# Computing the values of two dilated attention groups with the tokens stationary, in place of transposing them

## The reference, cut to what matters

```python
proj = h @ w_in                                   # h: 512 x 1024
qa, ka, va, za, qr, kr, vr, zr, ga, gr = jnp.split(proj, SPLIT_POINTS, axis=-1)
att_shape = (B, S, N_ATT_GROUPS, ATT_HEADS_PER_GROUP, ATT_HEAD_DIM)   # 3 groups, 4 heads, 128
...
for g, (window, dil) in enumerate(ATT_PATTERNS):  # (128,1), (512,4), (2048,16)
    o, lse = dilated_window_attention(qa[:, :, g], ka[:, :, g], va[:, :, g], window, dil)
```

## Time and profile before

| | before |
|---|---|
| median of 3 runs | 2590.46 us (2588.53 to 2593.51) |
| the profiled execution: time | 2593.51 us |
| the profiled execution: span, first to last instruction | 2591.7 us |
| granted TensorE clock, mean | 0.994 |
| busy: TensorE matmuls | 2564.2 us (99%), 13376 instructions |
| busy: weight loads | 2170.9 us (84%), 13376 instructions |
| busy: VectorE, ScalarE, GpSimd | 1157.5, 1045.2, 1135.2 us (45%, 40%, 44%) |

### The profile page before, as it was taken

One profiled execution on the slowest core, in us unless ns is written; L12 is line 12 of the kernel. 1 busy time (PEld: TensorE's weight loads), 2 busy tenths in 40 slices (PEclk: granted clock), 3 DMA queues, 4 the chain that ended last, 5 costly groups with the idle time before them and its releaser, 6 DMA issues.

```text
span 2591.7 us, 33239 instructions
## 1 busy us (share of the span) xinstructions
PE 2564.2 (99%) x13376; PEld 2170.9 (84%) x13376; DVE 1157.5 (45%) x2373; ACT 1045.2 (40%) x2006; POOL 1135.2 (44%) x663
## 2 busy tenths in 40 slices
PE   8999999999999999999999999999999999999998
PEld 8888877778888888889888888888898888888887
DVE  6572466556432694101333354542142345544313
ACT  3462376763234433223443333333243333333322
POOL 3354344444445455445344444444444444444342
PEclk9999999999999999999999999999999999999999
DMA  5133210105533354223222222222222222222222
GB/s 189 66 102 105 72 33 25 34 25 195 195 106 138 109 192 167 96 95 105 78 82 82 82 80 83 86 86 98 98 99 88 83 84 79 88 82 83 96 94 87
DMA packets 71769, 250.47 MB, mean 97 GB/s; under 512 B 7872, under 2 KB 12736, under 8 KB 71232
## 3 DMA queue, kind: packets, MB, share of 16 engines
q1 hardware_dynamic: 71616, 248.35, 28.4%
HBM read 246.22 MB, written 2.10 MB: 96 GB/s over the span
## 4 chain that ended last, share of the span: by engine, by line
PE 93%; DVE 4%; ACT 2%; DMA 0%; issue 0%; POOL 0%; DVEq 0%; SPq 0%
PE bank L1714 91%; PE bank L1724 3%; DVE XC L2241 1%; DVE rk_lo L2233 0%; DVE Ylo L2233 0%; DVE sq L2233 0%; ACT TR L1939 0%; ACT w_hi L1939 0%; DVE nt L2233 0%; DMA w_raw<-in_wa 0%; DVE Hlo L2233 0%; DVE nB L2233 0%; ACT Hhi L1939 0%; DMA XR<-in_x 0%; DVE blkk L2237 0%
## 5 line engine op out<-in xcount | busy, mean ns | idle before, releaser
L2769 POOL TENSOR_TENSOR w_lo<-w_raw,w_hi 128x1024 fp32r<-128x1024 f32 (+1 forms) x398 | 949.6, 2390 | 1137.7 <-ACT w_hi L1939 1137.3
L1714 PE MATMUL bank<-Hhi,w_hi 128*128 128x512 f32 (+1 forms) x2144 | 844.0, 394 | 1.4 <-DVE XC L2241 1.3
L1714 PE MATMUL bank<-Hlo,w_hi 128*128 128x512 f32 (+1 forms) x2144 | 825.0, 385 | 2.2 <-DVE Hlo L2233 0.8
L1714 PE MATMUL bank<-Hhi,w_lo 128*128 128x512 f32 (+1 forms) x2144 | 824.2, 384 | 0.0
L1939 ACT ACTIVATE w_hi<-w_raw 128x1024 fp32r<-128x1024 f32 (+1 forms) x398 | 408.0, 1029 | 163.1 <-DMA w_raw<-in_wa 118.1
L1714 PEld LDWEIGHTS bank<-Hhi,w_lo 128*128 128x128 f32 x2144 | 404.5, 189 | 81.3
L1714 PEld LDWEIGHTS bank<-Hhi,w_hi 128*128 128x128 f32 x2144 | 405.1, 189 | 79.8 <-issue 5.3
L1714 PEld LDWEIGHTS bank<-Hlo,w_hi 128*128 128x128 f32 x2144 | 405.5, 189 | 72.3 <-DVE Hlo L2233 3.0
L1714 PE MATMUL bank<-w_hi,Hhi 128*128 128x256 f32 (+2 forms) x384 | 117.6, 306 | 0.0
L1714 PE MATMUL bank<-w_hi,Hlo 128*128 128x256 f32 (+2 forms) x384 | 116.0, 302 | 0.0
L1714 PE MATMUL bank<-w_lo,Hhi 128*128 128x256 f32 (+2 forms) x384 | 115.9, 302 | 0.0
(11 more groups left out here) (355 smaller groups left out, 4264.6 us busy)
## 6 DMA issues: line engine op xcount, KB each, us to landing
w_raw<-in_wb SPq DMA_DIRECT2D x211, 512.0 KB, 3.4
w_raw<-in_wa SPq DMA_DIRECT2D x174, 512.0 KB, 3.4
wm<-in_w_ada SPq DMA_DIRECT2D x48, 512.0 KB, 4.4
wa_raw<-in_wb SPq DMA_DIRECT2D x5, 512.0 KB, 6.0
XR<-in_x SPq DMA_DIRECT2D x4, 512.0 KB, 6.5
w1k<-in_w1k SPq DMA_DIRECT2D x1, 2048.0 KB, 12.8
w1v<-in_w1v SPq DMA_DIRECT2D x1, 2048.0 KB, 17.7
XR<-in_x SPq DMA_DIRECT2D x1, 2048.0 KB, 8.3
```

What stands on the lines that cost most here:

```text
L1714: return self.e.matmul(o, lhs, rhs, start=start, stop=stop)
L2769: self.e.tensor_tensor(x.lo[:, k:k + n, :], x.raw[:, k:k + n, :], f(x.hi[:, k:k + n, :]), ALU.subtract).then_inc(*w_rest(s, k))
```

## The change

The values of groups 1 and 2 of a head are computed together by `product_t`, with 128 tokens of `H` stationary and the 256 weights of both groups moving. The stationary tokens are taken at a step of four, `x[:, r:512:4]`, which is a step of 16 bytes, so that the result of place r has the tokens r, r+4, ... on its partitions. The existing `in_rows` (`rows_split`) rounds it with ScalarE and subtracts with VectorE, straight from the bank to `vB12`. Group 0 keeps its product, copy and transposes. In the weights' layout the two tiles of one k now lie side by side. The values of the two groups have one signal, `("v12", L, hh, 3)`, where they had two.

```diff
-        def dilated_values(self, L, hh, H, free):
-            for g in (1, 2):
-                self.run(self.product(H, ("bv", L, hh, g), self.turned_to(L, hh, g, free)))
...
                 i2 = hh % 2
-                v_free = self.v_free[i2]
+                v12 = [vB12[i2][:, :, x, :, :].rearrange("p g t n -> p t g n") for x in range(2)]
+                dilated = self.product_t(H, ("v12", L, hh), 256, PAIRS,
+                                         self.in_rows(("v12", L, hh), *(lambda t, v=v: v[:, t, :, :] for v in v12), self.v_free[i2]),
+                                         lambda x, r: x[:, r:512:4])
                 if hh:
-                    self.dilated_values(L, hh, H, v_free)
+                    self.run(dilated)
                 for g in range(3 if hh else 0):
                     self.run(self.product(H, ("bk", L, hh, g), self.to_k(L, hh, g)))
                 for g in range(0 if hh else 1, 3):
                     self.run(self.product(H, ("bq", L, hh, g), self.to_q(L, hh, g)))
                 if hh == 0:
-                    self.dilated_values(L, hh, H, v_free)
-                self.run(self.product(H, ("bv", L, hh, 0), self.turned_to(L, hh, 0, v_free)))
+                    self.run(dilated)
+                self.run(self.product(H, ("bv", L, hh), self.turned_to(L, hh, self.v_free[i2])))
...
         def att_times_dilated(self, L, hh, x, k, ob, bank_free):
-            self.wait_ge(act_att.by("t", L, hh, x), dve_att.by("t", L, hh, x), dve_att.by("vt", L, hh, 1), dve_att.by("vt", L, hh, 2), bank_free)
+            self.wait_ge(act_att.by("t", L, hh, x), dve_att.by("t", L, hh, x), dve_att.by("v12", L, hh, 3), bank_free)
...
-        def v_copy(self, L, hh, g, i, o, points):
+        def v_copy(self, L, hh, i, o, points):
             self.wait_ge(*points)
-            if g == 0:
-                self.put(vfB[i][:, :], o).then_inc(*act_att("v", L, hh, g))
-            else:
-                self.put(vfB[i][:, :].rearrange("p (r t) -> p r t", r=4), o.rearrange("p (t r) -> p r t", r=4)).then_inc(
-                    *act_att("v", L, hh, g))
+            self.put(vfB[i][:, :], o).then_inc(*act_att("v", L, hh))
...
             kq, v = [x[h::4] for x in (ka, qa)], va[h::4]
-            v = [v[1:3]]
+            v = [v[1:3].transpose(1, 0, 2, 3)]
```

More of the change, by code:

```diff
@@ L1126, in in_rows, with turned_to @@
             return evac
-        def turned_to(self, L, hh, g, *points):
+        def turned_to(self, L, hh, *points):
             def evac(o, done, c):
@@ L1131, in evac @@
                 self.n_vf += 1
-                self.v_copy(L, hh, g, i, o, [done, self.vf_free[i]])
+                self.v_copy(L, hh, i, o, [done, self.vf_free[i]])
                 def turn():
@@ L1136, in turn @@
                     b = self.tb_.take()
-                    self.v_turn(L, hh, g, i, b, self.freed[b], points)
-                    self.vf_free[i] = att_turned.by("v", L, hh, g)
-                    self.freed[b] = [dve_att.by("vt", L, hh, g)]
+                    self.v_turn(L, hh, i, b, self.freed[b], points)
+                    self.vf_free[i] = att_turned.by("v", L, hh)
+                    self.freed[b] = [dve_att.by("v0", L, hh)]
                     yield 0
                 self.turns.append(self.later(turn()))
-                return [act_att.by("v", L, hh, g)]
+                return [act_att.by("v", L, hh)]
             return evac
-        def dilated_values(self, L, hh, H, free):
-            for g in (1, 2):
-                self.run(self.product(H, ("bv", L, hh, g), self.turned_to(L, hh, g, free)))
         def silu(self, key, dst, *points):
@@ L1630, in stat_parts @@
         return st, st[:, 96:104], st[:, 104:112], st[:, 112:120]
-    def value_rows(hh, g):
-        if g == 0:
-            return vB[hh % 2][0][:, :, :], vB[hh % 2][1][:, :, :]
-        return vB12[hh % 2][:, g - 1, 0, :, :], vB12[hh % 2][:, g - 1, 1, :, :]
     def dilated_sums(b, r):
@@ L1848, in cmp_times, with v_turn @@
             self.mm(o, vc[rows, gp, :], ct_lo[v % 2][rows, :], False, True).then_inc(*valued.named(*names))
-        def v_turn(self, L, hh, g, i, b, bank_free, points):
-            self.wait_ge(act_att.by("v", L, hh, g), bank_free)
+        def v_turn(self, L, hh, i, b, bank_free, points):
+            self.wait_ge(act_att.by("v", L, hh), bank_free)
             for s in range(TT):
                 ins = self.transpose(banks[b][:, 128 * s:128 * s + 128], vfB[i][:, 128 * s:128 * s + 128])
-            ins.then_inc(*att_turned("v", L, hh, g))
+            ins.then_inc(*att_turned("v", L, hh))
         def att_qk(self, L, hh, n, b, first, final, bank_free):
@@ L1892, in att_times_near @@
             i2, c = hh % 2, 0
-            self.wait_ge(act_att.by("t", L, hh, x), dve_att.by("vt", L, hh, 0), bank_free, dve_att.by("t", L, hh, x))
+            self.wait_ge(act_att.by("t", L, hh, x), dve_att.by("v0", L, hh), bank_free, dve_att.by("t", L, hh, x))
             for g, s, have in PACKS[x]:
@@ L2154, in rows_split, with v_turn @@
             self.put(hi, banks[b][:, :].rearrange("p (t g n) -> p t g n", t=2, g=2)).then_inc(*act_att(*key, t))
-        def v_copy(self, L, hh, g, i, o, points):
+        def v_copy(self, L, hh, i, o, points):
             self.wait_ge(*points)
-            if g == 0:
-                self.put(vfB[i][:, :], o).then_inc(*act_att("v", L, hh, g))
-            else:
-                self.put(vfB[i][:, :].rearrange("p (r t) -> p r t", r=4), o.rearrange("p (t r) -> p r t", r=4)).then_inc(
-                    *act_att("v", L, hh, g))
-        def v_turn(self, L, hh, g, i, b, bank_free, points):
-            self.wait_ge(att_turned.by("v", L, hh, g), *points)
-            self.put(value_rows(hh, g)[0], banks[b][:, :].rearrange("p (s n) -> p s n", s=TT)).then_inc(*act_att("vt", L, hh, g))
+            self.put(vfB[i][:, :], o).then_inc(*act_att("v", L, hh))
+        def v_turn(self, L, hh, i, b, bank_free, points):
+            self.wait_ge(att_turned.by("v", L, hh), *points)
+            self.put(vB[hh % 2][0][:, :, :], banks[b][:, :].rearrange("p (s n) -> p s n", s=TT)).then_inc(*act_att("v0", L, hh))
         def silu2(self, key, dst, o, points):
@@ L2611, in rows_split, with v_turn @@
             self.tt(lo, banks[b][:, :].rearrange("p (t g n) -> p t g n", t=2, g=2), f(hi), ALU.subtract).then_inc(*dve_att(*key, t))
[L2613 to L2616, removed]
+        def v_turn(self, L, hh, i, b, bank_free, points):
+            hi, lo = vB[hh % 2]
+            self.wait_ge(act_att.by("v0", L, hh))
+            self.tt(lo[:, :, :], banks[b][:, :].rearrange("p (s n) -> p s n", s=TT), f(hi[:, :, :]), ALU.subtract).then_inc(*dve_att("v0", L, hh))
         def silu2(self, key, dst, o, points):
```

## The result

The changed kernel takes 2674.43 us (median of 4 runs, 2674.21 to 2677.66) where the kernel before takes 2591.93 (4 runs, 2588.53 to 2593.51). The ratio is 1.0323, with a 95% interval of 1.0305 to 1.0341: slower by 82.5 us. The forecast was 2587, the range ended at 2642. Rival A's upper price, 2664, comes nearest.

A forecast was written before the change was run, and what follows sets the result against it. TensorE, busy for 99% of the span, was taken as the bound. Removed transposes, -7.2 us, and more but shorter matmuls, +3.8, gave -3.4 us: from the median of 2590.46 to 2587, range 2583 to 2642.

The forecast's parts named there:

- Rival A: Dilated values' `product_t`: the load at 16 bytes becomes TensorE's bound, +37 us (2627) or +74 (2664); 34 in 100.
- I take the contiguous price: New product's weight loads at a 16-byte step: as fast as contiguous ones, 0.113 us, hidden behind 256 columns at 0.120.
- The 0.78 ns an element: VectorE's reads of `Ek` at 32 bytes: at most this, against 0.88 ns a column that a load needs.
- The rows of `tmpB`: Reads and writes at 16 bytes by other engines: slower by 1.52 on VectorE, 1.95 for ScalarE's writes.
- the 0.007 us of margin: New product on TensorE: a load slot of 0.113 us hidden behind a matmul of 256 columns, 0.120 us.
- a rule that spoke against the change: Trainium skill on SBUF's 16-byte lines: readers need at least two hits a line; a 16-byte step gives one.
- -7.2 for the turns: Groups 1 and 2, 8 heads: 16 transposes of values (`v_turn`) removed from TensorE at 0.447 us each.
- +3.8 for the halved matmuls: Per head, 96 matmuls of 256 columns at 0.120 us replace 48 of 512 at 0.2264 or 0.2313.
- Nothing for ScalarE, VectorE, the slabs and banks 6 and 7: Work beside TensorE counted 0: ScalarE mostly idle, slabs keep their pace, the new banks have 5.4 us of air.
- Rival C: New product: fewer transpose pieces only open gaps for waits on banks 6 and 7; 2590 to 2594 us; 4 in 100.
- Rival B: First retention head of each layer: TensorE's waits for a late low part go, -4.9 us, 2585.6; 19 in 100.
- What would show it: Changed profile: `vfB` transposes 96 to 32, 256 more `w_hi,Hhi` matmuls, starts 0.120 us apart; 0.17 to 0.22 if loads are slower.

The follow-up runs named there:

- step1: The changed kernel with 128 neighbouring tokens stationary (a step of 4 bytes) instead of every fourth, for timing alone: 2588.2 us, ratio 0.9992.

## Why the prediction was wrong

- **The step that failed** is "I take the contiguous price" for the load whose columns lie 16 bytes apart. The slot is 0.2333 us, 2.07 times the 0.113 of the earlier trace rows. Every nanosecond above 0.120 was to cost 0.77 us, and that price was right: 113.3 ns x 0.768 = 87.0 us. No other term of the sum was wrong by more than the measurement can tell.
- **Why that price was taken.** It came from another engine, and from a row that was misread. The 0.78 ns an element of the earlier trace rows takes the whole duration of a short operation, 0.17 us, from the distance between two long ones, 0.26. The records overlap (they last 0.33), so a distance holds less of the fixed part than a duration does. By durations throughout, `Ek` took (334 - 170) / 116 = 1.41 ns an element, and contiguous operands of the same kind of operation (261 - 178) / 168 = 0.49: 124 elements at 32 bytes lasted longer than 192 in a row. The pattern differs in more than its step (four runs of 31), so how much of this is the step's isn't shown. But the row was no evidence that a wide step is free, and it stood alone on that side. The rows of `tmpB` were set aside because a load doesn't write, but nothing showed that the writing was what cost there. Measured on TensorE itself, the load needs 1.82 ns a line and the moving side 0.87. VectorE's groups in the kernel before, the reads of `Ek` and two contiguous operations (count, busy us, mean ns):

```profile
L2237 DVE TENSOR_SCALAR blkk<-Ek,par 128x124 f32<-128x124 f32 x16 | 4.2, 334 | 0.0
L2238 DVE TENSOR_SCALAR gate<-gate 128x192 f32<-128x192 f32 x1 | 0.3, 261 | 0.3 <-ACT gate L1939 0.3
L2237 DVE TENSOR_SCALAR gh<-par 128x24 f32<-128x24 f32 x1 | 0.2, 178 | 1.9 <-DMA par<-in_par 1.9
```

- **How the chances were dealt.** The prediction had the place (the 0.007 us of margin), the asymmetry (a faster load gains nothing, a slower one costs 0.77 us per ns) and a rule that spoke against the change. With a gain of 3.4 us on one side and 37 to 74 on the other, the unknown was the whole forecast, and 34 in 100 for it was too little. The range then left out A's upper price, the one nearest the truth.
- **Rival A** had the mechanism: the load as the bound of `product_t`, in the 96 matmuls of each head. Its upper factor, 1.95, from ScalarE's writes to `tmpB`, gave a slot of 0.220 and 2664 us; measured were 0.233 and 2674. The factor is that of another engine's writes, and no run ties it to the load's 2.07, so that it came so near is luck as far as is known.
- **-7.2 for the turns and +3.8 for the halved matmuls** hold together: step1 has both and no slow load, and took 2588.2 against 2590.62, -2.4 us with an interval from -4.4 to 0, where -3.4 was forecast. They were not measured apart.
- **Nothing for ScalarE, VectorE, the slabs and banks 6 and 7**: right. The even distances of the changed kernel and of step1 show no idle time at the new product. Rival C falls.
- **Rival B** falls too. The wait of the earlier trace rows is still there, in the changed kernel's timeline as the line below (0.58 us), and costs 0.72 to 0.75 us a layer over the even distance in this kernel and in step1.

```profile
1567.36 0.48 PE L1707 MATMUL bank<-tB,vB_hi 128*128 128x256 f32 x2 [0.58 <-DVE tB L2222]
```

- **What would show it**: the distance was named as the deciding sign, 0.120 or 0.17 to 0.22. It was 0.233, at a clock of 1.00. The counts came as said; in the changed kernel's groups (busy us, mean ns) the matmuls `w_hi,Hhi` of 256 columns are 544, 256 more, and the pieces of `vfB` 32 in place of the 96 of the earlier trace rows:

```profile
L1707 PE MATMUL bank<-w_hi,Hhi 128*128 128x256 f32 x544 | 184.5, 339 | 0.0
L1717 PEld LDWEIGHTS bank<-ident,vfB 128*128 128x128 f32 x32 | 4.0, 139 | 1.0
```

## What to carry to other kernels

A stationary operand with a step of 16 bytes takes twice the time to load; behind a matmul of 512 columns that is free, behind one of 256 it doubles the distance: before a transpose is traded for a strided load, ask how many columns follow each load, and put it clear of another task's short matmuls. An operation that the profile doesn't show should be priced by a row of the same engine and the same port. If no such row exists and the margin is small, the forecast is that unknown, and a row from another engine shouldn't decide it. Any row used as a price should be set against its contiguous twin, durations with durations and distances with distances.

## What the runs showed of the hardware

- Time of a weight load of 128 columns by the step of its operand, as the distance of starts behind 256 columns: 4 and 8 bytes 0.120 (set by the columns; the load alone is 0.113), 12 bytes 0.177, 16 bytes 0.233, 32 bytes 0.242. From 12 bytes up that is 1.82 to 1.89 ns for each 16-byte line.
- The moving operand at 16 bytes: 0.87 ns a column against 0.42.
- Behind a short matmul of 128 columns, a matmul of 512 takes 0.29 to 0.30 us to the next start with a contiguous load, and 0.40 with one at 16 bytes.
- The rule of the Trainium skill ("Advanced Engine Details and Errata", section "SBUF Cachelines") shows in both of TensorE's operands, where the size differs. VectorE's read at 32 bytes lasted longer than a contiguous one as well (1.41 ns an element against 0.49 by durations), but no run separates its step from the rest of its pattern.
- Left open: why 32 bytes cost 3.6% more than 16, and whether the price is for each line that is touched or for each change from one line to another. A load that comes back to the same lines in turn would tell; no run here has one.
